# Up projection by seven block products, down projection in a phase of its own

## The reference

```
def _conv_ffn(h, conv_prev, w_up, conv_w, conv_b, w_down):
    u = h @ w_up                                  # 1024 -> 2 x 2816 columns
    L = u.shape[1]
    ext = jnp.concatenate([conv_prev.astype(u.dtype), u], axis=1)
    c = conv_b + sum(conv_w[j] * ext[:, j:j + L] for j in range(FFN_CONV))   # FFN_CONV = 3
    gate, val = jnp.split(c, 2, axis=-1)
    return (jax.nn.silu(gate) * val) @ w_down, ext[:, -(FFN_CONV - 1):]

x = x + _merge(ya, yb, yc, gl, w_branch, w_out)
f, conv_new = _conv_ffn(_rmsnorm(x, norm_ffn), conv_prev, w_up, conv_w, conv_b, w_down)
x = x + f
```

## Time and profile before

| | us |
|---|---|
| median of 3 runs | 3207.99 (3206.93 to 3209.89) |
| the profiled execution, its own time | 3207.9 |
| its span, first to last instruction | 3206.1 |
| TensorE busy | 3100.3 (97%) |
| Vector engine busy | 1368.8 (43%) |
| ScalarE busy | 1132.8 (35%) |
| GpSimd busy | 864.5 (27%) |
| mean granted TensorE clock | 0.987 |

### The profile page before, as it was taken

The page is one execution under the profiler, slowest core; times in us unless marked ns, Lnnn a source line. Parts: engine busy times, 40 slices in busy tenths (PEclk is TensorE's granted clock), DMA queues, the critical chain, the costliest instruction groups (busy, mean ns, idle before and its releaser), DMA issues. The chain is left out here.

```text
span 3206.1 us, 49696 instructions
## 1 busy us (share of the span) xinstructions
PE 3100.3 (97%) x19550; PEld 2923.5 (91%) x19550; DVE 1368.8 (43%) x1448; ACT 1132.8 (35%) x1656; POOL 864.5 (27%) x524
## 2 busy tenths in 40 slices
PE   7899999999999999999998999999999999999997
PEld 6899999999988888888886879999999999999996
DVE  5554355444535455555542232122054444444443
ACT  5244334433334435444443331012242222222222
POOL 2333233323312121211212221343332322222320
PEclk8999999999999999999999999999999999999998
DMA  6312121121157778779777663432121111111101
GB/s 177 88 41 75 55 61 57 53 73 57 56 116 126 129 147 137 146 149 159 135 135 187 157 240 102 138 106 70 54 73 40 43 42 39 39 39 39 46 20 71
DMA packets 687890, 297.81 MB, mean 93 GB/s; under 512 B 350588, under 2 KB 668572, under 8 KB 687816
## 3 DMA queue, kind: packets, MB, share of 16 engines
q1 hardware_dynamic: 683368, 288.00, 37.7%
q10 hardware_dynamic: 4448, 8.80, 0.8%
HBM read 241.27 MB, written 55.46 MB: 93 GB/s over the span
## 5 line engine op out<-in xcount | busy, mean ns | idle before, releaser
L119 POOL TENSOR_TENSOR weight_lo<-weight_stage,weight_hi 128x1024 fp32r<-128x1024 f32 x180 | 449.8, 2500 | 1255.7 <-ACT weight_hi L114 1255.7
L2009 PE MATMUL group<-h_hi_part,weight_hi 128*128 128x384 f32 x1056 | 359.1, 340 | 6.3 <-DVE h_lo_part L2239 4.7
L2010 PE MATMUL group<-h_lo_part,weight_hi 128*128 128x384 f32 x1056 | 358.8, 340 | 0.0
L2011 PE MATMUL group<-h_hi_part,weight_lo 128*128 128x384 f32 x1056 | 358.8, 340 | 0.0
L166 PE MATMUL group<-h_hi_part,weight_hi 128*128 128x384 f32 x912 | 323.3, 355 | 15.3 <-DVE key_rows L764 5.0
L114 ACT ACTIVATE weight_hi<-weight_stage 128x1024 fp32r<-128x1024 f32 x180 | 190.9, 1061 | 413.9 <-PE group L2276 241.2
L167 PE MATMUL group<-h_lo_part,weight_hi 128*128 128x384 f32 x912 | 309.7, 340 | 0.0
L168 PE MATMUL group<-h_hi_part,weight_lo 128*128 128x384 f32 x912 | 309.5, 339 | 0.0
L1451 PE MATMUL group<-h_hi_part,weight_hi 128*128 128x384 f32 x768 | 267.9, 349 | 1.2 <-ACT next_v L1197 1.0
L1451 PE MATMUL group<-h_hi_part,weight_lo 128*128 128x384 f32 x768 | 261.2, 340 | 0.0
L2274 PE MATMUL group<-h_hi_part,weight_hi 128*128 128x384 f32 x768 | 258.8, 337 | 2.2 <-PEq L1621 2.2
(11 more groups left out here) (363 smaller groups left out, 6583.7 us busy)
## 6 DMA issues: line engine op xcount, KB each, us to landing
weight_stage<-in_w_in SPq DMA_DIRECT2D x88, 512.0 KB, 4.7
cached_v<-in_cache_diff_v SPq DMA_DIRECT2D x128, 256.0 KB, 5.2
cached_k<-in_cache_diff_k SPq DMA_DIRECT2D x224, 128.0 KB, 4.2
weight_stage<-in_w_up SPq DMA_DIRECT2D x44, 512.0 KB, 3.8
gate_in<-scratch_gates SPq DMA_DIRECT2D x24, 576.0 KB, 3.7
weight_stage<-in_w_branch SPq DMA_DIRECT2D x24, 512.0 KB, 4.1
down_stage<-in_w_down SPq DMA_DIRECT2D x22, 512.0 KB, 3.5
scratch_gates<-gate SPq DMA_DIRECT2D x16, 576.0 KB, 4.0
```

The source lines that it names most:

```text
L119: pool.tensor_tensor(self.wlo[:, n % 2, :], self.wst[:, n % 2, :], self.whi[:, n % 2, :].bitcast(F32), ALU.subtract).then_inc(self.w_lo, 1)
L2009: pe.matmul(o, w[0][:, k, :], ahi[:, k, rows], start=(k == 0), stop=False)
L2010: pe.matmul(o, w[0][:, k, :], alo[:, k, rows], start=False, stop=False)
L2011: last = pe.matmul(o, w[1][:, k, :], ahi[:, k, rows], start=False, stop=(k == KT - 1))
```

## The change

1. The up projection of one pair is a 2 x 2 block product: rows in halves of 576 (512 of the prompt and four streams), k in halves of 512, the columns being gate and value. In place of eight block products there are seven (`P1` to `P7`), of combined operands. The activation side has seven quadrants (A11, A12, A22 and the sums S1 to S4), made once, in parts hi and lo, before and during the first pair's turn. The weight side has four combinations of 128x512 for each pair (`combine`, Vector engine). Each product is 4 k x 2 chunks (256 and 320 columns) x 3 parts into two banks; there are four such accumulators in turn.
2. The products are put together in SBUF, in the buffers `gates` (two, in turn) and `value`: ScalarE copies P2 into the gate's first half (`m2`), P1 into the second (`m1`) and P5 into the value's second (`m5`); the Vector engine adds `c11`, `u2`, `c12`, `u3`, `c21`. The two sums that read no PSUM and go into the value, `u4` and `c22`, are GpSimd's.
3. The turn's order is P1, P5, P6, P3, P7, P2 of the next pair, P4. The gate taps of a pair run in the next turn. The gated products are stored to DRAM (`store_f`).
4. The down projection is a phase of its own: 66 steps, for each third of the rows (3 tiles of 128) all 22 k tiles. The stationary operand is the activations, the moving one 512 columns of w_down, so the result comes out with rows on the partitions; w_down is loaded three times. The residual x2 was stored to DRAM in the merge phase, comes back by thirds and is transposed between the steps, as are the new states.
5. The output projection writes the rows in the new order, over four banks (256, 320, 256, 320). 57 semaphores of earlier phases are allocated otherwise and cleared and freed at the start of `mem_phase` (`early_sem`).

The core of the diff:

```
+HR = ROWS // 2
+CHUNKS = ((0, 256), (256, 320))
...
+        def multiply(q, quad, arriving=None, at=0):
+            out = bank[q % 4]
+            wh, wl = (w.rearrange("p (k n) -> p k n", n=P) for w in slot(q))
+            xh, xl = X[quad]
+            for k in range(KH):
+                if arriving is not None:
+                    pe.wait_ge(arriving, at + k + 1)
+                for b, (c, n) in enumerate(CHUNKS):
+                    o, cols = out[:, b, 0:n], slice(c, c + n)
+                    pe.matmul(o, wh[:, k, :], xh[:, k, cols], start=(k == 0), stop=False)
+                    pe.matmul(o, wh[:, k, :], xl[:, k, cols], start=False, stop=False)
+                    last = pe.matmul(o, wl[:, k, :], xh[:, k, cols], start=False, stop=(k == KH - 1))
+            last.then_inc(prod, 1)
...
+        def turn(t, n):                                   # TensorE
+            t.wait(pe, S["c12_out"], 1, 0)
+            run(t, "P1", "A11", on_pool, 0)
+            t.wait(pe, S["u3_out"], 1, 0)
+            run(t, "P5", "S1", on_pool, KH)
+            t.wait(pe, S["m2_out"], 1, 1)
+            run(t, "P6", "S2", on_pool, 2 * KH)
+            t.wait(pe, S["c21_out"], 1, 0)
+            run(t, "P3", "S4", on_dve, KH)
+            t.wait(pe, S["m1_out"], 1, 1)
+            run(t, "P7", "S3", on_dve, 2 * KH)
+            t.wait(pe, S["m5_out"], 1, 1)
+            if n < FT - 1:
+                run(t, "P2", "A12")
+                t.wait(pe, S["u2_out"], 1, 1)
+            run(t, "P4", "A22", on_pool, 3 * KH)
...
+        def turn(t, n):                                   # ScalarE
+            if n:
+                operand_hi(act, t, 0, "P3")
+                tap0(t, -1, 0)
+                m1(t)
+                operand_hi(act, t, 0, "P7")
+                m5(t)
+                if n < FT - 1:
+                    operand_hi(act, t, 0, "P2")
+                silu(t, -1)
+            operand_hi(act, t, 0, "P4")
+            if n < FT - 1:
+                operand_hi(act, t, 1, "P1")
+                operand_hi(act, t, 1, "P5")
+            else:
+                down_hi(act, 0)
+                down_hi(act, 1)
...
+            tap0(t, 0, 1)
+            if n < FT - 1:
+                m2(t, 1)
+                operand_hi(act, t, 1, "P6")
...
+        def turn(t, n):                                   # Vector engine
+            c21(dve, t, -1)
+            c11(dve, t)
+            taps(dve, t, -1, 0)
+            if n < FT - 1:
+                combine(dve, t, 1, 1)
+                combine(dve, t, 1, 2)
+            u2(dve, t)
+            product(dve, t, -1)
+            c12(dve, t)
+            if n < FT - 1:
+                combine(dve, t, 1, 4)
+            u3(dve, t)
+            if n == FT - 1:
+                down_f_lo(dve, 0)
+                down_f_lo(dve, 1)
+            else:
+                combine(dve, t, 1, 3)
+            taps(dve, t, 0, 1)
+        turns(dve, turn)
+        t = Turn(FT)
+        c21(dve, t, -1)
+        taps(dve, t, -1, 0)
+        down_f_lo(dve, 2)
+        product(dve, t, -1)
...
+        def turn(t, n):                                   # GpSimd
+            pads(t, 0, 1)
+            news(t, -1, 0)
+            operand_lo(pool, t, 0, "P3")
+            operand_lo(pool, t, 0, "P7")
+            if n < FT - 1:
+                operand_lo(pool, t, 0, "P2")
+                pads(t, 1, 0)
+            operand_lo(pool, t, 0, "P4")
+            u4(pool, t)
+            if n < FT - 1:
+                operand_lo(pool, t, 1, "P1")
+                operand_lo(pool, t, 1, "P5")
+            else:
+                down_w_lo(0)
+            c22(pool, t)
+            news(t, 0, 1)
+            if n < FT - 1:
+                operand_lo(pool, t, 1, "P6")
+            else:
+                down_w_lo(1)
...
+        def turn(t, n):                                   # SyncE
+            if n <= FT - 3:
+                wait_op(sp, lo_r, t, 0, "P4")
+                load_pair(sp, t, 2, 0)
+                load_pair(sp, t, 2, 1)
+            if n:
+                store_f(sp, t, -1)
+            if n == FT - 1:
+                wait_op(sp, prod, t, 0, "P5")
+                for s in range(3):
+                    load_step(sp, s)
...
+    def u4(pool, t):
+        t.wait(pool, S["m5_out"], 1, 1)
+        t.wait(pool, S["u2_out"], 1, 1)
+        add_out(pool, "u4_out", value, 0, held(value, 1), held(gates[t.n0 % 2], 1))
...
+    def c22(pool, t):
+        t.wait(pool, S["u3_out"], 1, 1)
+        add_out(pool, "c22_out", value, 1, held(value, 1), held(gates[t.n0 % 2], 1))
...
+        for s in range(STEPS):                            # TensorE, down, STEPS = 3 * FT
+            gi, k = s // FT, s % FT
+            pe.wait_ge(dn.S["down_w_lo"], s + 1)
+            pe.wait_ge(dn.S["down_f_lo"], s + 1)
+            for m in range(3):
...
+                for h in range(2):
+                    cols = slice(h * 512, (h + 1) * 512)
+                    wh, wl = dn.whi[:, s % 3, cols], dn.wlo[:, s % 3, cols]
+                    pe.matmul(acc[:, h, :], fh, wh, start=(k == 0), stop=False)
+                    pe.matmul(acc[:, h, :], fl, wh, start=False, stop=False)
+                    last = pe.matmul(acc[:, h, :], fh, wl, start=False, stop=(k == FT - 1))
```

More of the change, by code:

```diff
@@ L1994, in mem_phase @@
     g.first.close()
-def up_product(pe, ps, w, ahi, alo, free):
-    pe.wait_ge(*free)
-    for k in range(KT):
-        last = up_step(pe, ps, w, ahi, alo, k)
-    return last
-def up_step(pe, ps, w, ahi, alo, k):
-    for bank in range(NC):
-        o, rows = ps[:, bank, 0:CW], slice(bank * CW, (bank + 1) * CW)
-        pe.matmul(o, w[0][:, k, :], ahi[:, k, rows], start=(k == 0), stop=False)
-        pe.matmul(o, w[0][:, k, :], alo[:, k, rows], start=False, stop=False)
-        last = pe.matmul(o, w[1][:, k, :], ahi[:, k, rows], start=False, stop=(k == KT - 1))
-    return last
@@ new lines, in by_chunk, with chunk_banks, __init__, wait @@
+def by_chunk(ap):
+    v = ap.rearrange("p (h n) -> p h n", h=2)
+    return v[:, :, 0:256], v[:, :, 256:HR]
+def chunk_banks(ps):
+    v = ps[:, 0:4, :].rearrange("p (h c) n -> p h c n", h=2)
+    return v[:, :, 0, 0:256], v[:, :, 1, 0:320]
+class Turn:
+    def __init__(self, n0, i=0):
+        self.n0, self.i = n0, i
+    def wait(self, eng, sem, per, k):
+        const = self.n0 * per + k
+        if const > 0:
+            eng.wait_ge(sem, self.i * (4 * per) + const)
+    def pair(self, d, at=0):
+        return ds(self.i * 4 + (self.n0 + d + at), 1)
@@ L2164, in _, with x2 @@
             act.wait_ge(mlo_r, KT)
-            with act.Fori(0, LOOPS) as i:
+            def x2(i, c):
+                ps = R.ready(act, names[c], i)
+                act.wait_ge(acc_r, i * 2 + (c + 1))
+                for dst, part in zip(by_chunk(sq[:, c, :]), chunk_banks(ps)):
+                    last = act.activation(dst, part, ACT.Square)
+                last.then_inc(sq_r, 1)
+                for dst, part in zip(by_chunk(tile(i, c)), chunk_banks(ps)):
+                    last = act.activation(dst, part, ACT.Copy)
+                R.freed(last, names[c])
+            with act.Fori(0, LOOPS - 1) as i:
                 for c in range(2):
-                    ps = R.ready(act, names[c], i)
-                    act.wait_ge(acc_r, i * 2 + (c + 1))
-                    act.activation(tiles(sq[:, c, :]), ps[:, 0:NC, 0:CW], ACT.Square).then_inc(sq_r, 1)
-                    R.freed(act.activation(tiles(tile(i, c)), ps[:, 0:NC, 0:CW], ACT.Copy), names[c])
+                    x2(i, c)
                     g.round_w(act, 2 + c, i, NW)
+            for c in range(2):
+                x2(LOOPS - 1, c)
+            ffn["first_parts_act"](act)
             for v, ts in enumerate(vec_tiles[:EARLY]):
@@ L2270, in product @@
                         pe.wait_ge(arriving, at + k + 1)
-                    for n in range(NC):
-                        cols = slice(n * CW, (n + 1) * CW)
-                        o = ps[:, n, 0:CW]
+                    for n, (c, width) in enumerate(banks):
+                        cols = slice(c, c + width)
+                        o = ps[:, n, 0:width]
                         pe.matmul(o, wh[:, k, :], ahi[:, k, cols], start=(k == 0 and open_sum), stop=False)
```

1132 lines of the change are left out of this document (702 added, 430 removed).

## The result

The changed kernel takes 3230.53 us in the median of 4 runs (3228.18 to 3232.25), the kernel before 3208.94 (3206.93 to 3210.94, 4 runs): a ratio of 1.0065, 95% interval 1.005 to 1.008. The profiled execution has a span of 3226.4 us and took 3228.18. So the change makes this kernel slower by 0.65%, though TensorE has 62 us less to do from the norm's factor on by the prediction's count.

A forecast was written before the change was run, and what follows sets the result against it. Bound: exclusive SBUF use by Vector engine and GpSimd, 23.7 us a turn against TensorE's 22.4. Start 2329.0, up phase 589.2, down 269.3 + 14.0 + 9.4 + 4, last tile 8.1: span 3223.0, plus 1.8 outside, 3224.8 us; range 3188 to 3262.

The forecast's parts named there:

- Semaphores: Start of the memory phase: clearing 57 semaphores adds 3 us, with bounds 0 and 6.
- First turn: From the norm's factor to P1 of turn 1: 64.5 us, as Vector and GpSimd work make TensorE's 25.6 us wait.
- half clock there costs nothing: First turn: TensorE at half clock adds no time, since the products have the time.
- Turns: Twenty turns of one pair each: 24.8 us per turn, with 1.25 us per 512-element GpSimd instruction.
- Changeover: Up to down phase: step 0 28.7 us after turn 21 starts, 5 after the last product; steps 2 and 3 lose 9.4.
- Down phase: 66 steps of 4.08 us, 269.3 in all; transposes 14.0, waits 9.4 and half clock 4 us.
- Last tile: End of the kernel: sum, squares, rstd and product 5.0 us, store 3.1, together 8.1.
- (a): Rival for the turns: the hold hardly costs and TensorE bounds them at 22.4 us, total 3152; chance 0.07.
- (b): Rival for the turns: cheaper GpSimd pieces, 23.2 us per turn gives 3192; chance 0.15.
- (c): Rival: GpSimd's strided sums and 576-wide rests cost more, or nothing passes during a hold; turns 26.3, total 3262; chance 0.16.
- (d): Rival: TensorE's clock falls within the turns, some bound at half clock, total 3290 or more; chance 0.05.
- walk of the queues: Stepping four queues through a turn with waits and holds: closing path 24.7 us, 22.4 without the hold.

The follow-up runs named there:

- e3: Changed kernel with the third of three matmuls (weights' rest times rounded activations) left out of the up products, rests still made: 3230.59 us, single run.
- e2: Changed kernel with GpSimd's weight-operand rests written as zeros by memset, only two columns still subtracted: 3162.8 us, single run.
- e8: Changed kernel with c11 reading P1 from PSUM, still behind m1: 3222.81 us, ratio 1.0036 to the kernel before.
- e5: Changed kernel with c11 reading P1 from PSUM ahead of m1 and both sums (u4, c22) on the Vector engine: 3164.59 us, ratio 0.9865.
- e7: e5 plus the first down loads and the parts for down steps 2 and 3 issued earlier: 3156.80 us, ratio 0.9839.
- e1: Changed kernel with both sums (u4, c22) moved from GpSimd to the Vector engine: 3218.06 us, ratio 1.0017.
- e4: Changed kernel with c11 reading P1 from PSUM, ahead of m1: 3200.75 us, ratio 0.9964.
- e9: Changed kernel with GpSimd's sixteen 576-wide quadrant rests of the first turn written as zeros, two columns still subtracted: 3213.08 us, ratio 1.0007.

## Why the prediction was right, point by point

**The mechanism.** The bound by the two engines' exclusive use, with TensorE waiting in each turn, is what the runs show: e3 takes a third of TensorE's work away for nothing, e2 takes GpSimd's reading away and gets 22.33. e8 takes one hold away and leaves the order, for 0.45 us a turn; e5 leaves every rest in place, only moves the two sums and lets c11 read PSUM, and gets 22.33 too. The Trainium skill (SBUF — State Buffer, Who interferes with whom) says that a Vector instruction with two inputs in SBUF contends with a GpSimd instruction that reads SBUF, not with one that only writes it. The trace agrees, with taps of 2.2 to 2.5 us beside rests and of 1.43 us under a memset. The Trainium skill says in the same section (SBUF — State Buffer, Who interferes with whom) that issue order decides who blocks. The trace agrees: in e7 either engine is held by what the other had begun before it.

**The time.** 3225 was forecast, 3230.5 measured. The terms, in the profiled execution (span 3226.4 for 3223.0):

| term | forecast | measured |
|---|---|---|
| norm's factor first used | 2329.0 | 2324.75 |
| to P1 of turn 1 | 64.5 | 67.0 |
| twenty turns | 496 | 503.7 |
| turn 21 to down step 0 | 28.7 | 28.4 |
| down phase | 296.7 | 292.9 |
| last tile | 8.1 | 9.7 |

- **Semaphores**, 3 us: nothing that shows. TensorE's idle time ahead of the first matmul of the memory phase is 8.08 us, before 8.15, and the matmul starts at 1692.23, before at 1692.19. The lower bound fits. The start alone could not tell 3 us: in the twelve traces with the same code up to there it lies between 1690.65 and 1696.84, and the norm's factor between 2322.42 and 2331.03. So the 4.3 us of the table's first row lie within the spread from one execution to the next.
- **First turn**: 2.5 too short. By the forecast P4 would start 61.3 us after the norm's factor (64.5 less its own 3.2), and it starts after 62.2, 0.9 late. The other 1.6 are the clock: P4 starts behind a wait of 4.33 us, runs at half clock until 2390.2 and takes 4.8 us. So the prediction's "half clock there costs nothing" was wrong for this last product.

```profile
2386.96 0.55 PE L2814 MATMUL group<-A_hi,weight_hi 128*128 128x256 f32 x1 [4.33 <-issue]
```

```profile
2386.90:2390.20 3.30, 3.24 (x14) 3.27 (x15) 2.19 (x2) 0.64 (x1) 3.30 (x3) 0.50 0.71 206
```

- **Turns**, 24.8: they take 25.19. The 512-element rests of GpSimd take 1.29 us free, not 1.25; the prediction itself gave 25.0 for 1.30. But the steady turns take 25.5, as the first two and the last two are shorter, so 0.5 us a turn stays unexplained.
- **Changeover**: the wait ahead of step 0 is 2.99, not 5, since the load of step 0 was issued at 2915.49 behind the store and the up products ended only at 2920.8. The total of 28.4 fits because turn 21 itself is as much longer.
- **Down phase**: the waits ahead of steps 2 and 3 come to 3.78 and 1.11, 4.9 and not 9.4; half clock cost 4.8 us and not 4 (the three steps before step 3, with the wait ahead of it, take 22.0 us, 9.7 over 3 x 4.08, of which 4.9 are the waits). Step 3 doesn't wait for ScalarE long, as the store's product is done at 2940.7. The steps of 4.08 are as forecast, the transposes and what goes with them take 13.9 of 14 (271.0 from step 3 to the last matmul, less 63 x 4.08).
- **Last tile**: 1.6 too short. The last tile's addition waits behind the row product of the tile two before it, as the Vector engine's queue shows, and then square, rstd and row product follow:

```profile
3217.41 1.28 DVE L2587 SCALAR_TENSOR_TENSOR x_rows<-x_rows,x_rstd_col,norm_final_row 128x1024 f32<-128x1024 f32 x1 [0.77 <-POOL x_rstd_col L2729]
3218.61 1.21 DVE L2582 TENSOR_TENSOR x_rows<-x_rows,group 128x1024 f32<-128x1024 f32 x1
...
3221.95 1.28 DVE L2587 SCALAR_TENSOR_TENSOR x_rows<-x_rows,x_rstd_col,norm_final_row 128x1024 f32<-128x1024 f32 x1 [0.93 <-POOL x_rstd_col L2729]
```

The deviations are both ways, -4.3 + 2.5 + 7.7 - 0.3 - 3.8 + 1.6 = 3.4, so the small miss owes something to luck. A slip in the prediction's sums changes nothing in this: its own chances add up to 0.23 for faster and 0.61 for slower, not 0.24 and 0.60.

**The rivals.** (a), the hold hardly costs, fell with the turns of 25.5, though its 22.33 is real: e2 and e5 reach it. (b) and (c) bracket the 25.2; (c)'s claim that nothing passes during a hold fell, as in the prediction's own rows. (d), a falling clock within the turns, did not happen in the changed kernel (1.00 in the window); in e3, where TensorE waits up to 3.7 us at a time, the clock is 0.87.

**Where the walk of the queues failed.** It gave the changed kernel's turn within 0.4 us of the mean and e1's 25.0 (25.1 in the walk), but for c11 from PSUM it gave 23.0 where 24.2 was measured. With the sums too I added the gains up to 23.7, and 22.33 was measured. A likely reason, argued and not shown, is that handovers which the prediction put at 0.05 to 0.2 us decide whether two holds meet, and are not known well enough. Why just these holds meet in e4 and not in e5 was read from the timelines, not tested by shifting one instruction alone; that stays open. So does how much of the 22.6 us that e9's first turn still takes beyond TensorE's 25.6 is order, and how much is hold.

## What to carry to other kernels

Saving work on the engine that bounds a stage pays only down to the next bound, and that need not be an engine: here it is a closed path through two queues that exclude each other, at busy shares of 74% and 61%. Add up what must not overlap before moving work to GpSimd, keep additions' operands in PSUM where they are there anyway, and let an operand be read before a copy of it is made. The gain of removing one hold can't be added to that of another: here the pair of edits worth 0.45 and 1.25 us a turn gave 3.1 together, so try them together before dropping either.
